# A twelfth weight piece ahead in each expert phase: two residual tiles parked in memory, quarters issued before the gather

## The reference

```python
def expert_choice_moe(x, w_router, b_router, w_gate, w_up, w_down):   # E = 16 experts, cap = 64 tokens each
    aff = softmax(x @ w_router + b_router)
    gate, idx = top_k(aff.transpose(0, 2, 1), cap)
    xs = x[bidx, idx]                                                   # the gather
    hid = silu(xs @ w_gate) * (xs @ w_up)                               # per expert, 1024 x 1024 each
    ys = (hid @ w_down) * gate
    return zeros_like(x).at[bidx, idx].add(ys)                          # the scatter
x = x + expert_choice_moe(rms_norm_2(x, norm_ffn), ...)
```

## Time and profile before

| | us |
|---|---|
| runs shown | 2521.20, 2523.14, 2523.38 (median 2523.14) |
| the profiled execution, its own time | 2521.9 |
| its span | 2519.8 |

### The profile page before, as it was taken

The page is one execution under the profiler, slowest core; times in us unless marked ns, Lnnn a source line. Parts: engine busy times, 40 slices in busy tenths (PEclk is TensorE's granted clock), DMA queues, the critical chain, the costliest instruction groups (busy, mean ns, idle before and its releaser), DMA issues.

```text
span 2519.8 us, 26913 instructions
## 1 busy us (share of the span) xinstructions
PE 2442.7 (97%) x10855; PEld 1523.6 (60%) x10855; DVE 1229.2 (49%) x2148; ACT 462.0 (18%) x986; POOL 123.2 (5%) x204
## 2 busy tenths in 40 slices
PE   8999999999999999999999999889999999999899
PEld 4458888888888888786653333333576553333333
DVE  4667898755766554556741222111756641121112
ACT  3432121002322100324610000000125510000000
POOL 1301110000000000001100000000001000000000
PEclk9999999999999999999999999999999999999999
DMA  8635775551443324313159999999431359999998
GB/s 310 213 109 182 269 245 161 159 145 39 134 134 109 92 67 118 117 65 134 68 213 387 428 427 427 427 428 419 147 123 76 125 195 426 426 427 427 427 428 355
DMA packets 189595, 605.38 MB, mean 240 GB/s; under 512 B 10416, under 2 KB 124544, under 8 KB 164384
## 3 DMA queue, kind: packets, MB, share of 16 engines
q1 hardware_dynamic: 172592, 548.46, 56.4%
q0 software_dynamic: 15584, 50.95, 5.9%
q10 hardware_dynamic: 1296, 4.25, 0.4%
HBM read 597.34 MB, written 6.29 MB: 240 GB/s over the span
## 4 chain that ended last, share of the span: by engine, by line
PE 79%; DMA 15%; DVE 3%; SPq 1%; issue 1%; ACT 1%; DVEq 0%; ACTq 0%
DMA arena<-in_w_down 14%; PE ps L2320 11%; PE ps L2928 10%; PE ps L2445 7%; PE ps L2968 7%; PE ps L2331 6%; PE ps L2827 4%; PE ps L2645 4%; PE ps L2289 4%; PE ps L2605 3%; PE ps L2236 2%; PE ps L2356 2%; PE ps L2214 2%; PE ps L2979 2%; PE ps L2762 1%; PE ps L2563 1%
## 5 line engine op out<-in xcount | busy, mean ns | idle before, releaser
L2320 PE MATMUL ps<-arena 128*128 128x256 f32 x1280 | 278.0, 379 | 0.0
L2320 PEld LDWEIGHTS ps<-arena 128*128 128x128 f32 x1280 | 242.5, 190 | 33.7 <-issue 1.1
L2928 PE MATMUL ps<-arena,first 128*64 128x512 f32 x1024 | 231.4, 593 | 10.3 <-DMA arena<-in_w_up 10.3
L2928 PE MATMUL ps<-arena 128*64 128x512 f32 x1024 | 233.7, 598 | 0.5 <-DMA arena<-in_w_up 0.3
L2968 PE MATMUL ps<-arena 128*64 128x512 f32 x892 | 207.0, 620 | 24.7 <-DMA arena<-in_w_down 23.4
L2445 PE MATMUL ps<-arena 128*128 128x256 f32 x896 | 193.8, 379 | 0.1
L2445 PEld LDWEIGHTS ps<-arena 128*128 128x128 f32 x896 | 170.1, 190 | 23.6 <-issue 0.5
L2928 PEld LDWEIGHTS ps<-arena,first 128*64 128x64 f32 x1024 | 73.2, 137 | 159.7 <-issue 137.3
L2968 PEld LDWEIGHTS ps<-arena 128*64 128x64 f32 x892 | 67.3, 142 | 161.6 <-issue 159.8
L2928 PEld LDWEIGHTS ps<-arena 128*64 128x64 f32 x1024 | 73.7, 137 | 139.5 <-issue 131.9
L2331 PE MATMUL ps<-arena 128*128 128x256 f32 x672 | 146.0, 379 | 0.0
(11 more groups left out here) (491 smaller groups left out, 3245.3 us busy)
## 6 DMA issues: line engine op xcount, KB each, us to landing
arena<-in_w_gate SPq DMA_DIRECT2D x64, 2048.0 KB, 36.3
arena<-in_w_up SPq DMA_DIRECT2D x64, 2048.0 KB, 35.1
arena<-in_w_down SPq DMA_DIRECT2D x54, 2048.0 KB, 34.3
arena<-in_ffn_w SPq DMA_DIRECT2D x24, 2048.0 KB, 10.1
arena<-in_w_mod POOLq DMA_DIRECT2D x80, 512.0 KB, 5.0
arena<-in_ffn_w SPq DMA_DIRECT2D x32, 1024.0 KB, 7.5
arena<-in_w_in SPq DMA_DIRECT2D x10, 1536.0 KB, 10.3
arena<-in_w_down SPq DMA_DIRECT2D x12, 1024.0 KB, 37.9
```

The costliest lines, as they stand in the source:

```text
L2320: ins = mm(ps[:, i % 6, 0:256], src[:, k, P * j:P * j + P], x[:, k, :], start=(k == 0), stop=(k == 3))
L2928: ins = mm(ps[CAP * half:CAP * half + CAP, bank, :], xsT[q][:, k, CAP * (e % 2):CAP * (e % 2) + CAP], wv[:, k, 512 * half:512 * half + 512 ...
```

## The change

In each expert phase:

1. Piece 11 is loaded entirely ahead. Its quarters k = 0 and 1 go into the room of `x_tok` tiles 0 and 1, quarter 2 into `ahead` and `oh`, quarter 3 into the two `ye` tiles. Piece 12 then takes the slot of piece 0, in four quarters; the later pieces follow in `ORDER` shifted by one, so from piece 23 on each waits, as before, for the use of the piece eleven before it.
2. The two residual tiles are parked: ACT writes them to memory (`x_half`) ahead of its saves of `xn`. SP waits for both, then loads quarters 0 and 1 of piece 11, and only then pieces 8 and 9.
3. Piece 10 comes in quarters. Three of them wait for the saves of `xn` but not for the gather, the fourth waits for the gather. Quarter 2 of piece 11 is issued behind it.
4. At the end of the phase, behind the last weight load, SP fetches the parked rows (1024 KB) into the slot of piece 88. DVE adds them to `x_tok` (one operation of 128 x 2048, `parked_rows`) between the scaling of the last pair's two `ye` halves. The first pair's scatter writes tiles 0 and 1 with a copy where it had added.
5. DVE builds the first `oh` only after `outer(0)`, since `oh` holds weights until then.

```diff
+        AHEAD_AT = {0: ((x_tok[:, 0, :], 0, 1024),), 1: ((x_tok[:, 1, :], 0, 1024),), 2: ((ahead, 0, 512), (oh, 512, 1024)),
+                    3: ((ye[0], 0, 512), (ye[1], 512, 1024))}
+        x_park = nc.dram_tensor("x_half", (2 * P, D), F32, kind="Internal").ap()
+        def x_back(s):
+            return ring2[s][:, 0:2 * D].rearrange("p (t d) -> p t d", t=2)
...
         def loads_before(s, n):
-            return sum(1 for i in range(n) if ORDER[i % 11] == s)
+            return sum(1 for i in range(n) if i != AHEAD and ORDER[(i - (i > AHEAD)) % 11] == s)
...
                         sp.wait_ge(sm[name], value)
-                        if s == 9:
-                            sp.wait_ge(got[0], 16 * (8 * l + 1))
...
-                    if n == 11:
-                        for k in range(3):
-                            c0 = 512 if k == 2 else 0
-                            sp.wait_ge(r2_used[s], free - 3 + k)
-                            sp.dma_start(ring2[s][:, 1024 * k + c0:1024 * k + 1024], half.rearrange("(p k) n -> p k n", k=4)[:, k, c0:]).then_inc(r2_in[s], 16)
+                    if n == 10:
+                        for k in range(QUARTERS):
+                            if k == QUARTERS - 1:
+                                sp.wait_ge(got[0], 16 * (8 * l + 1))
+                            sp.dma_start(ring2[s][:, 1024 * k:1024 * k + 1024], half.rearrange("(p k) n -> p k n", k=4)[:, k, :]).then_inc(r2_in[s], 16)
+                        return
+                    if n == AHEAD + 1:
+                        for k in range(QUARTERS):
+                            sp.wait_ge(r2_used[s], free - QUARTERS + 1 + k)
+                            sp.dma_start(ring2[s][:, 1024 * k:1024 * k + 1024], half.rearrange("(p k) n -> p k n", k=4)[:, k, :]).then_inc(r2_in[s], 16)
                         return
...
-                def load_ahead():
-                    s, _, _, landed_at = expert_load(l, 0)
-                    sp.wait_ge(r2_in[s], landed_at)
-                    sp.wait_ge(sm["x_added"], 24 * l + 24)
+                def load_ahead(k):
                     half = a["w_down_2"][l, 1][512:1024, :].rearrange("(p k) n -> p k n", k=4)
-                    for dst, k, c0 in ((ahead, 2, 0), (ye[0], 3, 0), (ye[1], 3, 512)):
-                        sp.dma_start(dst, half[:, k, c0:c0 + 512]).then_inc(r2_in[s], 16)
+                    for dst, c0, c1 in AHEAD_AT[k]:
+                        sp.dma_start(dst, half[:, k, c0:c1]).then_inc(ahead_in, 16)
...
                 for n in range(LOADS - 4):
+                    if n == 8:
+                        sp.wait_ge(parked, 16 * (l * (R2_LANDS[9] + slot_total(9)) + 2))
+                        sp.wait_ge(sm["xn_done"], 8 * l + 2)
+                        sp.wait_ge(sm["lgp_ps"], 4 * l + 2)
+                        load_ahead(0)
+                        load_ahead(1)
                     if n == 10:
-                        load_ahead()
-                    load(n)
+                        sp.wait_ge(sm["x_added"], 24 * l + 24)
+                        load_ahead(3)
+                    if n != AHEAD:
+                        load(n)
+                    if n == 10:
+                        sp.wait_ge(sm["idx_cols"], 3 * l + 3)
+                        load_ahead(2)
...
                     load_rest(LOADS - 2 + par, last_cols_in[par], 512, D)
+                back, _, free, _ = expert_load(l, load_number(EXPERTS - 1, 0))
+                sp.wait_ge(r2_used[back], free)
+                sp.dma_start(x_back(back), x_park.rearrange("(t p) d -> p t d", p=P)).then_inc(back_in, 16)
...
+                def park(t):
+                    act.dma_start(x_park.rearrange("(t p) d -> p t d", p=P)[:, t, :], x_tok[:, t, :]).then_inc(parked, 16)
...
+                park(0)
                 save_normed(0)
...
+                park(1)
                 save_normed(1)
...
-                        V.tensor_tensor(x, ps[:, MO_BANK[n % 4], :], x, add).then_inc(sm["mo_added"], 1)
+                        if i == 0 and t < 2:
+                            V.tensor_copy(x, ps[:, MO_BANK[n % 4], :]).then_inc(sm["mo_added"], 1)
+                        else:
+                            V.tensor_tensor(x, ps[:, MO_BANK[n % 4], :], x, add).then_inc(sm["mo_added"], 1)
+                def parked_rows():
+                    s = expert_load(l, load_number(EXPERTS - 1, 0))[0]
+                    dve.wait_ge(back_in, 16 * (l + 2))
+                    dve.wait_ge(sm["mo_added"], 64 * l + 8 * (EXPERTS // 2 - 1))
+                    x = x_tok[:, 0:2, :]
+                    chain(V.tensor_tensor(x, x, x_back(s), add))
...
                     if i == 0:
                         dve.wait_ge(sm["iota_in"], 16 * (l + 1))
+                        dve.wait_ge(sm["ye_ps"], 3 * l + 1)
...
                         V.tensor_scalar(ye[half], ps[:, YE_BANK[half], :], gate_t[:, i:i + 1], None, mul).then_inc(sm["ye_done"], 1)
+                        if i == EXPERTS // 2 - 1 and half == 0:
+                            parked_rows()
```

More of the change, by code:

```diff
@@ L286, in program @@
         first_half_in = sm["out_saved"]
+        back_in, parked, ahead_in = sm["out_saved"], r2_in[9], r1_in[2]
         PARTS = ((0, 0, 512), (1, 0, 256), (1, 256, 512), (2, 0, 256), (3, 0, 256), (2, 256, 512), (3, 256, 512), (4, 0, 512))
@@ L368, in program @@
         IN_LANDS = {0: 2, 1: 2, 2: 3, 3: 1, 4: 1, 10: 1}
[L369 removed]
+        R2_LANDS = (3, 2, 3, 1, 2, 2, 0, 0, 0, 2, 1)
         ORDER = (10, 2, 1, 4, 3, 8, 7, 5, 0, 6, 9)
         LOADS = 6 * EXPERTS
[L372 removed]
+        QUARTERS, AHEAD, AHEAD_PARTS = 4, 11, 6
         def loads_before(s, n):
[L375 removed]
+            return sum(1 for i in range(n) if i != AHEAD and ORDER[(i - (i > AHEAD)) % 11] == s)
         def expert_load(l, n):
[L378 removed]
+            s = ORDER[(n - (n > AHEAD)) % 11]
             k = loads_before(s, n)
[L380 to L384, removed]
+            uses, total, more = slot_uses(s), slot_total(s), QUARTERS - 1 if s == ORDER[0] else 0
+            return (s, l * uses + k + (more if k else 0), l * uses + k + 1 + more,
+                    16 * (l * (R2_LANDS[s] + total) + R2_LANDS[s] + k + 1 + (more if k else 0) + (QUARTERS - 1 if s == ORDER[10] else 0)))
         def slot_total(s):
[L387 removed]
+            return loads_before(s, LOADS) + (QUARTERS - 1 if s in (ORDER[0], ORDER[10]) else 0)
         def slot_uses(s):
@@ L2929, in inner @@
                                          start=(q == 0 and k == 0), stop=(q == 1 and k == 3))
-                            if e == 0 and part + q == 0 and k < 3:
+                            if e == 0 and part + q == 0 and k < QUARTERS - 1:
                                 ins.then_inc(used, 1)
@@ L2939, in outer_last @@
                             if ks[0] and half == 0:
-                                pe.wait_ge(r1_in[2 - 2 * q + par], R1_TOTAL[2 - 2 * q + par] + 16 * (l + 1))
+                                pe.wait_ge(r1_in[2 - 2 * q + par], R1_TOTAL[2 - 2 * q + par] + 16 * (l + 1) * (AHEAD_PARTS + 1 if (q, par) == (0, 0) else 1))
                             elif ks[0] and q:
@@ L2956, in outer @@
                     for q in range(2):
-                        w = [piece(2 * i + par, 4 + q) for par in range(2)]
+                        w = [piece(2 * i, 4 + q)]
+                        if i == 0 and q == 1:
+                            pe.wait_ge(ahead_in, R1_TOTAL[2] + 16 * (l * (AHEAD_PARTS + 1) + AHEAD_PARTS))
+                        else:
+                            w.append(piece(2 * i + 1, 4 + q))
                         for k in range(4):
@@ L2961, in outer @@
                                 for par in range(2):
-                                    wv = w[par][0][:, k, 512 * half:512 * half + 512]
-                                    if (i, q, par) == (0, 1, 1):
-                                        if k == 3:
-                                            wv = ye[half]
-                                        elif (k, half) == (2, 0):
-                                            wv = ahead
+                                    if par < len(w):
+                                        wv = w[par][0][:, k, 512 * half:512 * half + 512]
+                                    else:
+                                        parts = AHEAD_AT[k]
+                                        wv = parts[half][0] if len(parts) == 2 else parts[0][0][:, 512 * half:512 * half + 512]
                                     ins.append(mm(ps[CAP * par:CAP * par + CAP, YE_BANK[half], :], hT2[par][:, k, CAP * q:CAP * q + CAP],
                                                   wv, start=(q == 0 and k == 0), stop=(q == 1 and k == 3)))
-                        for par in range(2):
-                            ins[par].then_inc(w[par][1], 1)
+                        ins[0].then_inc(w[0][1], 1)
+                        ins[1].then_inc(w[1][1] if len(w) == 2 else sm["ye_ps"], 1)
                 def scattered(i, t):
```

10 lines of the change are left out of this document (5 added, 5 removed).

## The result

The changed kernel takes **2531.48 us** (median of 7 runs, 2528.65 to 2532.95), the one before on the same chip 2521.67 (7 runs, 2520.72 to 2523.38): a ratio of 1.0035, with the 95% interval 1.0025 to 1.0045. It is slower by 0.35%, where 0.2% faster was forecast. The profiled execution took 2532.95 us, its span is 2531.1 against 2519.8 before: 11.3 us more. It was the slowest of the seven, and the medians differ by 9.8, so some 1.5 of the 11.3 come from which executions were profiled.

The account below looks back on a forecast made before the run. Each expert phase was taken as bound by DMA, the weight bytes after PE sets the unbroken stream's start. Layer sums -2.7 and -2.6, together -5.3 from 2523.14, gave 2517.9 us, range 2512.5 to 2525.

Parts of the forecast that it names:

- the gather: Start of each expert phase: three quarters sent ahead delay the gather PE waits for, +0.9 us a layer, bounds 0 and 6.9.
- the saves: Before the gather: the last save of `xn` lands up to 2.2 us later, about +0.3 us showing a layer.
- the stores: End of layer 1: scatter adds come closer together, so little queues; +0.2 us, once, bounds 0 and 0.5.
- Rival 1: At the gather: it is held as the pair's was, 6.9 in place of 0.9 us a layer, 2529.9; chance 0.11.
- The twelfth piece: Weight stream of each expert phase: one piece of 2048 KB less to carry, -4.9 us a layer, the whole gain.
- The rows that come back: End of each layer: fetching and adding parked rows delays the first scatter add, +1.0 us in layer 0, +0.9 in layer 1.
- Parking: Ahead of the first saves: two writes of 512 KB in the idle stretch, 0; without that stretch 2.5 us.
- Layer 1's inputs: Start of layer 1: inputs land 2.5 us later against the weights' end but PE has cover, 0; without it 1.5.
- Rival 2: Nothing collides: quarters through before the gather reads, parked rows in by 2509.1; -9.8 us, 2513.3; chance 0.18.
- Rival 3: End of each layer: parked rows come back late, 2.3 us a layer; -2.7 in all, 2520.4; chance 0.14.
- Rival 4: Long queue turns: the gather waits for two quarters' shares, 2.9 in place of 0.9 us a layer, 2521.8; chance 0.08.
- Rival 5: Late saves or parks put the three quarters behind the gather; stream only 1.8 us shorter a layer, 2522.3; chance 0.05.

Follow-up runs that it names:

- run 2: The changed kernel with all four quarters of piece 10 behind the gather: 2523.28 us, ratio 1.0001 to the kernel before.
- 3: The changed kernel with one quarter of piece 10 ahead of the gather and three behind it: 2524.12 us, ratio 1.0007 to the kernel before.
- run 5: The changed kernel with 18 filler matmul calls ahead of the gather where there were 7: 2525.83 us, ratio 1.0017 to the kernel before.
- Run 4: The kernel before without its 7 filler matmul calls ahead of the gather: 2523.30 us, ratio 1.0005 to the kernel before.
- run 6: The changed kernel with 29 filler matmul calls ahead of the gather where there were 7: 2534.28 us, ratio 1.0047 to the kernel before.
- run 10: The changed kernel with pieces 8 and 9 loaded in quarters with 4 KB rows: 2526.77 us, ratio 1.0021 to the kernel before.
- Run 8: The changed kernel, all quarters behind the gather, eleven filler calls, parked rows added after the second half's scaling: 2522.41 us, ratio 0.9999 to the kernel before.
- run 9: The changed kernel with its three early quarters sent as six transfers of 2 KB rows: 2528.02 us, ratio 1.0026 to the kernel before.
- run 1: The kernel before with only piece 10 in quarters, three ahead of the gather; no parking, no twelfth piece: 2530.60 us, ratio 1.0032 to the kernel before.
- run 7: The changed kernel with all quarters behind the gather and eleven filler matmul calls: 2523.05 us, ratio 1.0003 to the kernel before.

## Why the prediction was wrong, step by step

The forecast for two layers was -5.3; the spans say +11.3. The difference of 16.6 is made up of 5.3 for the gather, 10.2 for the stream (9.8 shorter forecast, 0.4 longer measured), 1.0 for the saves and 0.1 for the stores.

**The gather: +7.1 measured for +1.8.** This is the step that failed, and it failed in the sum and in the chances. I had priced it "packet for packet", from the turns that a *save* gets, with "some 3 packets accepted before it". But the queues of after show no turns at first: four microseconds with no packet of q0 at all. What SP's queue had been handed before went first. The bound from the other side was in my own text, the pair's gather at 10.6 against 3.7, and the hold grows with the bytes that SP's queue still has to move (runs 2, 3 and the change). I chose between far ends by the row that fitted my mechanism; the pair's gather was the nearer one: the same queue and kind of transfer, behind the same queue of SP. I had fitted its 10.6 us with turns of packets, but its own window in the kernel before shows none in its first 4.1 us, from 1344.65 to 1348.75:

```profile
q1 hardware_dynamic: 125, 1.79, 101.8%
```

From there on the two queues did share. So the wait for the first packet could be read before the change, 4.1 us in a full stream against 1.7 on idle engines. My sum had another flaw: it took three packets accepted ahead for the pair and only two for the gather; with three it would have said 1.1 and not 0.9, which changes little. Rival 1 had the right place and sign, but not its size: 3.5 a layer, just under the 3.6 from which I had said it decides the sign alone.

**The clock: never in the sum, +7.7 to +9.3 by the streams of one execution, 6.5 by the medians.** I wrote that a longer gather "is paid in full" and stopped there. PE's idle time went from 0.65 to 4.92 us, and the lower clock that follows costs 2.8 us in the first piece. The 2.5 us of the second stretch, 38 us later, hang on the gather only in part: PE had just waited for 0.78, 0.88 and 0.69 us for DVE and ACT, as it does there in the other kernels, and run 5, without the long wait, still has a slow stretch of 3.4 us there, which costs 1.7. Run 4 shows the first stretch without any held gather, run 5 takes it away with the gather still held. By run 5's streams it is 4.8 + 2.8 us; by those of run 6, 4.5 + 4.7. That is 7.7 to 9.3 of the stream's 10.2; the rest isn't explained. The rows needed for the warning stood in the profile of before: the fillers themselves, and a half-clock stretch of 3.4 us in its layer 0. The Trainium skill ("TensorE: Matmul & The Clock Gate", part 1) describes a gate that halves the clock by how busy the engine has been, and the traces agree as to the half (0.50 in the window above).

**The twelfth piece: right in kind.** It was forecast at -4.9 a layer, and with the first pieces at full clock it is -4.9 and -2.3 in run 5, -4.6 and -4.3 in run 6. The check that I had named, the stretch shorter by 4.9, failed in after itself, for the most part because the clock gave the time back. Why run 5's layer 1 has 2 us less than run 6's is open; PE began later against the bytes in run 6, and that is argued only. The sum also took 426 GB/s for all bytes. From 1334 to 1346 the engines of run 5 were as busy (0.98 to 1.01) but moved only 364 to 369 GB/s; there go the quarters of pieces 10 and 12 in 4 KB rows. No run tries what this costs.

**The saves: +0.3 a layer forecast, +0.6 and +1.1 measured.** The mechanism, a fifth of the bytes against 16 KB rows, was right; run 10 took it away and got 2.38 and 2.69 back. Two things were sized wrong. In layer 0 the last save landed 12.9 us after its issue (11.2 before), at 1323.1 and within the 1323.8 of the sum, but POOL issued the gather only at 1323.94, 0.8 us behind that landing (1.0 in layer 1), and the sum had nothing for this step. In layer 1 the save slipped by more than the 2.2 allowed, 13.5 us against 10.6.

**The rows that come back: right.** +1.0 and +0.9 forecast, +1.1 and +0.8 measured, with the add's 2.29 us and the wait for a DMA that I had put at 1.4 (DVE, end of layer 0, then of layer 1):

```profile
1768.11 0.75 DVE L2111 TENSOR_SCALAR arena<-ps,arena 128x512 f32<-128x512 f32 x1 [11.49 <-PE ps L2988]
1770.47 2.29 DVE L2072 TENSOR_TENSOR arena<-arena 128x2048 f32<-128x2048 f32 x1 [1.60 <-DMA arena<-x_half]
...
2520.20 2.29 DVE L2072 TENSOR_TENSOR arena<-arena 128x2048 f32<-128x2048 f32 x1 [1.45 <-DMA arena<-x_half]
```

Run 8 says that 0.3 to 0.45 a layer of it was avoidable by the order of two operations. The **stores** cost 0.3 for my 0.2.

**What I priced at nothing was nothing.** Parking, with 2.6 us to landing, ended in the idle stretch; "to ready" is 1321.00 against 1321.14. Layer 1's inputs did come late, and DVE waited for them, but "to layer 1's ready" is 292.96 against 292.94:

```profile
1789.29 1.83 DVE L1694 TENSOR_TENSOR arena<-arena 128x1600 f32<-128x1600 f32 x1 [1.42 <-DMA arena<-in_w_uq]
```

**The rivals.** Rival 1 happened for half its price and the clock doubled it. Rival 2 needed two margins of about 1 us, and neither held: the quarters met the gather, and DVE waited for the rows. Rival 3 did not occur, the tail kept its price. Rival 4's hold, two quarters' shares, was 2.9 where 3.5 came. That is close, but in rival 4 the queues take turns from the start, and the trace has none before the first 4.5 us are over. The Trainium skill ("DMA: Bandwidth & Descriptors", "Queues, rings and completion order") has each engine go round the queues packet by packet; in after, a stretch of 315 packets of one queue passed before the other's first. No run here shows whether POOL's packets were already waiting at the engines in that time, or were still being made. Rival 5's arithmetic came near in run 2, where I made it happen: -1.8 a layer by the bytes, -2.9 and -1.5 measured.

**What stays open.** What keeps back the gather's first packet: the rows of SP's queue that wait at the engines, or the making of the gather's own descriptors beside them. Neither a fixed number of bytes nor of rows fits: ahead of q0's first packet SP's queue moved 125 packets, mostly of 16 KB, for the pair of the kernel before, some 310 of 4 KB in the change and some 400 of 2 KB in run 9. Row size plays a part (run 9), and so does the amount (2, 3 and the change). An issue well ahead helps only if nothing stands before it in SP's queue: it did in layer 1 of run 1 (5.6 us) and not in run 10.

## What to carry to other kernels

A bulk transfer handed over just ahead of a small one that TensorE waits for is paid twice: in the small one's landing, here 1.0 us for 512 KB and 3.5 for 1536, and it can be in the clock behind the wait, here nearly as much again. The second price isn't always due: the slow first piece of run 2 left no gap in the DMA stream, and taking it away in run 7 gained nothing; in run 4 the medians don't show it either. So price a wait of TensorE with the matmuls that follow it, look whether the DMA stream behind gets a gap, and let filler matmuls last as long as the wait does and no longer. And where two rows of the profile give far-apart prices for a collision, take the one with the same queue and the same kind of transfer.

## What the runs showed of the hardware that I had not expected

- A gather issued behind 1536 KB on another queue got its first packet 4.5 us after its issue, against 1.7 on idle engines. The pair's gather in the full stream of the kernel before waited 4.1. With the same rows in 2 KB pieces the first packet came after 3.3, but the landing hardly sooner (6.3 for 7.4).
- Idle times of TensorE of 1.9 to 5.4 us ahead of the expert phase (runs 2 and 4, the change) were followed by granted clocks of 0.50 over 3.4 to 10.2 us, at some 1.2 to 2.8 us a time. Idle times of 0.4 to 1.0 us at the same place (run 5, the kernel before) were followed by 1.00.
- Two queues of 16 KB and 4 KB rows shared by rows; when both had 4 KB rows (run 10), the last save landed in 9.5 us instead of 12.9.
- With the DMA engines as busy, SP's pieces in 4 KB rows moved at 364 to 369 GB/s (run 5, 1334 to 1346) and those in 16 KB rows at 424 to 427.
